# Key pages loaded whole over 128 partitions, and turned probabilities sorted by position on TensorE

## The reference

```python
def _sample_attention(l, q, k_new, v_new, qi, ki_new, wi, cache_k, cache_v, cache_kidx, page_table):
    ...
    scores = _index_scores(qi, wi, ki_all)
    qpos = past + jnp.arange(T)
    causal = jnp.arange(L)[None, :] <= qpos[:, None]
    scores = jnp.where(causal[None], scores, -jnp.inf)
    _, idx = lax.top_k(scores, topk)            # topk = 256 of 1028 positions
    ...
    k_sel = jnp.where(is_past, cache_k[l, phys_page, offset].astype(k_new.dtype), k_new[bidx, nidx])
    v_sel = jnp.where(is_past, cache_v[l, phys_page, offset].astype(v_new.dtype), v_new[bidx, nidx])
    return _sparse_attend(q, k_sel, v_sel, valid)

def _sparse_attend(q, k_sel, v_sel, valid):
    s = jnp.einsum('bthd,btkhd->bthk', q, k_sel) * (HEAD_DIM ** -0.5)
    s = jnp.where(valid[:, :, None, :], s, -jnp.inf)
    p = jax.nn.softmax(s, axis=-1)
    return jnp.einsum('bthk,btkhd->bthd', p, v_sel)
```

## Time and profile before

| | |
|---|---|
| median of three runs | 1252.48 us (1248.2 to 1258.6) |
| the profiled execution | 1256.65 us, span 1254.8 us |
| PE busy | 1146.8 us (91%) |
| DVE, ACT, POOL busy | 641.2, 318.7, 354.4 us |
| mean granted TensorE clock | 0.953 |
| moved by DMA | 171.53 MB, mean 137 GB/s |

### The profile page before, as it was taken

One profiled execution on the slowest core, in us unless ns is written; L12 is line 12 of the kernel. 1 busy time (PEld: TensorE's weight loads), 2 busy tenths in 40 slices (PEclk: granted clock), 3 DMA queues, 4 the chain that ended last, 5 costly groups with the idle time before them and its releaser, 6 DMA issues.

```text
span 1254.8 us, 29323 instructions
## 1 busy us (share of the span) xinstructions
PE 1146.8 (91%) x11340; PEld 1065.1 (85%) x11340; DVE 641.2 (51%) x1173; ACT 318.7 (25%) x593; POOL 354.4 (28%) x150
## 2 busy tenths in 40 slices
PE   6999999999999999999957878887887899999995
PEld 6988889999999999999947767777766789999992
DVE  3566658875475575624554434624622752232326
ACT  4333334223233322323211111111111242212110
POOL 2433323333343343334202131121220313333320
PEclk8999999999999999999988988888889899999996
DMA  7542142332332333354049997997999958222203
GB/s 242 137 106 77 48 121 69 93 85 77 86 106 81 86 91 96 89 139 119 24 113 253 255 211 191 242 225 196 239 210 224 244 169 261 83 84 80 70 0 143
DMA packets 201900, 171.53 MB, mean 137 GB/s; under 512 B 22034, under 2 KB 182730, under 8 KB 200562
## 3 DMA queue, kind: packets, MB, share of 16 engines
q1 hardware_dynamic: 188410, 161.41, 49.3%
q10 hardware_dynamic: 13376, 8.53, 2.3%
HBM read 159.57 MB, written 9.90 MB: 135 GB/s over the span
## 4 chain that ended last, share of the span: by engine, by line
PE 70%; SPq 11%; DMA 8%; DVE 6%; issue 5%; ACT 1%; DVEq 0%; ACTq 0%
PE acc L1132 58%; SPq L454 4%; DMA kPage<-in_cache_k 4%; SPq L502 3%; DMA hist<-in_state_pool 3%; PE bank L1190 2%; PE bank L1307 1%; DVE scoreP L1755 1%; PE bank L1326 1%; DVE top L1751 1%; PE acc L1459 1%; PE bank L1432 1%; PE acc L1545 1%; SPq L457 1%; DMA xnat<-in_x_prompt 1%
## 5 line engine op out<-in xcount | busy, mean ns | idle before, releaser
L659 POOL TENSOR_TENSOR wL<-rawW,wH 128x1024 fp32r<-128x1024 f32 (+1 forms) x146 | 354.2, 2428 | 853.3 <-ACT wH L681 853.3
L1132 PE MATMUL acc<-actH,wH 128*128 128x272 f32 (+1 forms) x2304 | 499.1, 298 | 19.7 <-ACT raw L1005 16.2
L1132 PE MATMUL acc<-actH,wL 128*128 128x272 f32 (+1 forms) x2304 | 481.8, 291 | 0.0
L1132 PE MATMUL acc<-actL,wH 128*128 128x272 f32 (+1 forms) x2304 | 481.2, 291 | 0.0
L1132 PEld LDWEIGHTS acc<-actH,wH 128*128 128x128 f32 (+1 forms) x2304 | 366.7, 191 | 50.7 <-issue 49.0
L1132 PEld LDWEIGHTS acc<-actL,wH 128*128 128x128 f32 (+1 forms) x2304 | 367.4, 191 | 0.0
L1132 PEld LDWEIGHTS acc<-actH,wL 128*128 128x128 f32 (+1 forms) x2304 | 364.8, 191 | 0.0
L681 ACT ACTIVATE wH<-rawW 128x1024 fp32r<-128x1024 f32 (+1 forms) x146 | 153.3, 1054 | 269.5 <-PE acc L1132 235.0
L1860 DVE STREAM_TRANSPOSE kPage<-kPage 128x1024 f32<-128x1024 f32 x30 | 37.4, 1246 | 135.4 <-DMA kPage<-in_cache_k 135.3
L2095 DVE SCALAR_TENSOR_TENSOR y<-y,bank 128x512 f32 (+1 forms) x16 | 11.0, 688 | 123.3 <-PE bank L1609 121.4
L1432 PE MATMUL bank<-kPage,qBlock 128*32 128x64 f32 x1920 | 38.7, 239 | 31.1 <-DVE kPage L1861 27.2
(11 more groups left out here) (210 smaller groups left out, 906.6 us busy)
## 6 DMA issues: line engine op xcount, KB each, us to landing
rawW<-in_w_in SPq DMA_DIRECT2D x112, 512.0 KB, 3.9
vPage<-in_cache_v SPq DMA_DIRECT2D x64, 512.0 KB, 9.3
kPage<-in_cache_k SPq DMA_DIRECT2D x112, 256.0 KB, 6.4
rawW<-in_w_out SPq DMA_DIRECT2D x32, 512.0 KB, 3.9
y<-in_x_prompt SPq DMA_DIRECT2D x4, 1024.0 KB, 8.6
out_y_prompt<-y SPq DMA_DIRECT2D x8, 512.0 KB, 2.8
xnat<-in_x_prompt SPq DMA_DIRECT2D x2, 1024.0 KB, 8.3
xnat<-in_x_prompt ACTq DMA_DIRECT2D x2, 1024.0 KB, 11.5
```

Source lines behind the costliest of these rows:

```text
L659: pool.tensor_tensor(wL[:, slot, :, 0:width], rawW[:, slot, :, 0:width], wH[:, slot, :, 0:width].bitcast(F32), ALU.subtract).then_inc(stag ...
L1132: last = pe.matmul(acc[t.slot][0:width, e, 0:HT], w[:, u.slot, k, 0:width], a[:, kk, e * HT:(e + 1) * HT], start=(half == 0 and k == 0 and ...
```

## The change

A key page is loaded whole, one DMA over all 128 partitions as a value page is, so a unit is two DMAs in place of four, and both page numbers are read before the wait for the buffer. Side s now holds positions 32 s to 32 s + 31 of each page. The scores of page p so stand in columns 32 p to 32 p + 31 of `probS`, with the sides on rows. `dropD` is written to match, in runs of 32 numbers rather than 128. The two transposes of the probabilities become 32 products: for page p and side s the stationary operand is the 32 columns of page p, the moving operand 32 columns of the identity that pick the rows of side s, and the result goes to partitions 32 s to 32 s + 31. `probST` is then position by page by row, and `value_page` reads its four columns from there.

Three things are moved. The first two units of "a" are taken in the order 1, 0, and DVE turns them earlier, between softmaxes of the last two heads. SP issues a half-tile of weights (`unit(4)`) ahead of the mask instead of behind it. SP issues `pool_loads(0)` right behind the first mask, ahead of the wait for `c_done` and of the first values and keys.

```diff
 BLOCK = QUARTERS * SIDES * STREAK
+FIRST = (1, 0, 2, 3)
 TRI = [0, 128, 384, 768, 1280]
...
             probSTn = sb("probSTn", [NS, P], F32, s)
-            probST = sb("probST", [P, 2, P], F32, s)
+            probST = sb("probST", [P, PAGES, NS], F32, s)
             pooledS = sb("pooledS", [P, 2, NS], F32, s)
...
             uN = hist[0:NS]
-            outS = probST[:]
+            outS = probST[:].rearrange("p a t -> p (a t)").rearrange("p (a d) -> p a d", a=HALF)
             qAll = mixed[:, KC - 2:KC, :].rearrange("p k t -> p (k t)")[:, 0:SIDES * H * NS].rearrange("p (j n) -> p j n", j=SIDES)
...
             def first_key_part(unit, e):
-
-                dst, at = first_keys(unit, e), STREAK * (2 * (unit % 2) + e)
-                for side in range(SIDES):
-                    page = page_number(ck, SIDES * (unit // 2) + side)
-                    sp.dma_start(dst[STREAK * side:STREAK * (side + 1), :],
-                                 ck[ds(page, 1), at:at + STREAK, :].rearrange("a p n -> p (a n)")).then_inc(first_k_in[unit], 16)
+                load_page(ck, first_keys(unit, e), page_number(ck, 2 * unit + e), first_k_in[unit])

...
                 i, at = (0, 0) if g is None else (g, g)
+                pages = [page_number(ck, (2 * at + x) * PAGES + (2 * n + e)) for e in range(2)]
                 sp.wait_ge(k_done, 2 * UNITS * i + done)
-                for side in range(SIDES):
-                    page = page_number(ck, (2 * at + x) * PAGES + (SIDES * (n // 2) + side))
-                    rows_of = ck[ds(page, 1), 2 * STREAK * (n % 2):2 * STREAK * (n % 2 + 1), :]
-                    sp.dma_start(kPage[STREAK * side:STREAK * (side + 1), 1 - n % 2, :, :, :].rearrange("p e h d -> p e (h d)"),
-                                 rows_of.rearrange("a (e p) n -> p (a e) n", e=2)).then_inc(k_in[n % 2], 16)
+                for e in range(2):
+                    load_page(ck, kPage[:, 1 - n % 2, e, :, :].rearrange("p h d -> p (h d)"), pages[e], k_in[n % 2])

...
                 for a in range(HALF):
-                    sp.dma_start(dropD[side, a, :, 0:HP].rearrange("r (h n) -> r h n", h=2),
-                                 scoreS[:, 0:PAST].rearrange("r (h s n) -> r h s n", h=2, s=SIDES)[:, :, side, :]
+                    sp.dma_start(dropD[side, a, :, 0:HP].rearrange("r (p n) -> r p n", p=PAGES),
+                                 scoreS[:, 0:PAST].rearrange("r (p s n) -> r p s n", p=PAGES, s=SIDES)[:, :, side, :]
                                  ).then_inc(drop_out, 16)
...
                          outside[0:NS, 0:NS].unsqueeze(1).to_broadcast([NS, (SIDES - 1) * HALF, NS])).then_inc(drop_out, 16)
-            mask(0, None)
             unit(4)
+            mask(0, None)
+            pool_loads(0)
             sp.wait_ge(c_done, 1)
...
             value_page(0, 0)
-            key_unit(1, 0, 1)
+            key_unit(1, 0, FIRST.index(0) + 1)
             value_page(0, 1)
             unit(5)
-            pool_loads(0)
             value_page(0, 2)
...
                     src = bank_wait(act, b)
-                    act.activation(probST[:].rearrange("p a r -> p (a r)"), src[:, 0:2 * P], ACT.Copy)
+                    act.activation(probST[:].rearrange("p a r -> p (a r)"), src[:, 0:PAGES * NS], ACT.Copy)
                     out_of(b, probSTn[:], src[0:NS, 2 * P:3 * P])
...
                 i, x, b = 0 if g is None else g, "abc".index(X), bb(f"S{X}", g)
-                pe.wait_ge(k_turned, 2 * UNITS * i + UNITS * x + n + 1)
-                if n == 0:
+                at = n if x else FIRST.index(n)
+                pe.wait_ge(k_turned, 2 * UNITS * i + UNITS * x + at + 1)
+                if at == 0:
                     pe.wait_ge(pad_ready, 2 * i + x + 1)
...
             copied(TILE_C + 31)
-            for n in range(UNITS):
+            for n in FIRST:
                 key_products("a", n)
...
                     stand_alone(pe)
-                    for n in range(2):
-                        pe.transpose(dst[:, n * P:(n + 1) * P], probS[:, n * P:(n + 1) * P], ident)
+                    for p in range(PAGES):
+                        for side in range(SIDES):
+                            pe.matmul(dst[STREAK * side:STREAK * (side + 1), p * NS:(p + 1) * NS], probS[:, p * STREAK:(p + 1) * STREAK],
+                                      ident.rearrange("p (j s r) -> p j s r", j=QUARTERS, s=SIDES)[:, :, side, :],
+                                      start=True, stop=True)
                     full(b, pe.transpose(dst[0:NS, 2 * P:3 * P], probS[:, HP:LP], ident))
...

-                    def column(h, side):
-                        at = h % QUARTERS * SPAN + (side * HALF + h // QUARTERS) * NT
+                    def column(h, step):
+                        at = h % QUARTERS * step + h // QUARTERS * NT
                         return slice(at, at + NT)
...
                     for h in range(H):
-                        end = products(h, probST[:, p // SIDES, column(h, p % SIDES)], vPage[:, v.slot, h, :], p == 0, False)
+                        end = products(h, probST[:, p, column(h, HALF * NT)], vPage[:, v.slot, h, :], p == 0, False)
                     end.then_inc(v_free[v.slot], 1)
...
                         for h in range(H):
-                            end = products(h, probSTn[:, column(h, 0)], vS[:, h, :], False, True)
+                            end = products(h, probSTn[:, column(h, SPAN)], vS[:, h, :], False, True)
                         full(o, end)
...
                 if X == "a":
-                    dve.wait_ge(first_k_in[n], 16 * 2 * SIDES)
+                    dve.wait_ge(first_k_in[n], 32)
                     parts = [first_keys(n, e) for e in range(2)]
                 else:
-                    dve.wait_ge(k_in[n % 2], 16 * SIDES * (4 * i + 2 * (x - 1) + n // 2 + 1))
+                    dve.wait_ge(k_in[n % 2], 32 * (4 * i + 2 * (x - 1) + n // 2 + 1))
                     parts = [kPage[:, 1 - n % 2, e, :, :].rearrange("p h d -> p (h d)") for e in range(2)]
...
                     rotated(1, qT, 0, i)
+                if late:
+                    keys_turned("a", FIRST[0])
                 softmax(0)
...
                     rotated(3, qT, 1, i)
+                    if late:
+                        keys_turned("a", FIRST[1])
                     gated(0, (2, 3))
...
                     own.wait()
-                    keys_turned("a", 0)
                     queries(0)
-                    keys_turned("a", 1)
-                    keys_turned("a", 2)
                 if i:
...
                         own.wait()
-            keys_turned("a", 3)
+            for n in FIRST[2:]:
+                keys_turned("a", n)
             dve.wait_ge(c_done, 1)
```

More of the change, by code:

```diff
@@ L581, in _ @@
                          outside[0:NS, 0:NS].unsqueeze(1).to_broadcast([NS, (SIDES - 1) * HALF, NS])).then_inc(drop_out, 16)
+            unit(4)
             mask(0, None)
-            unit(4)
+            pool_loads(0)
             sp.wait_ge(c_done, 1)
```

## The result

The changed kernel took **1175.45 us** (median of 4 runs, 1175.03 to 1180.29) against 1253.22 us (median of 4 runs, 1248.2 to 1258.6) of the kernel before: ratio 0.9403, 95% interval 0.9359 to 0.9448. The forecast was 1182. Its forecast was 1186.65. Ratios are of fast runs alone: in the experiments a few runs of the kernel before lie over 1.5% above its fastest and are left out of them.

The account below looks back on a forecast made before the run. It took the DMA engines as fullest, PE next. Waits and clock 58 plus start 17 minus sorting 5 gave 70 us off the profiled 1256.65, so 1186.65; the forecast median was 1182, range 1162 to 1220.

Parts of the forecast that it names:

- The cause: Sample stage: a key byte loaded over 32 partitions costs the DMA engines twice a value byte, 208 against 407 GB/s.
- The waits: PE's waits in the groups shrink: 23 us at key products, 10 at later groups' history, 15 at new accumulators.
- The slow clock: Six quarter tiles after waits, slow at a low granted clock: 10 us of 11.9 us regained.
- The start: Start of the sample stage: mask and history come sooner, PE begins the first group near 647, not 665.3: 17 us.
- Sorting: Turns of the probabilities on PE: 32 small products replace two transposes, eight times, costing 5 us; bounds 2 and 117.
- the rule on drains: Skill's rule that changing the tiling mode drains TensorE: two more drains a sorting turn would make 5 us about 7.
- Small pieces: Dropped scores, eight DMAs writing 128-byte instead of 512-byte pieces: cost 1 us, inside the start's 17; bounds 0 and 27.
- The key turns among the softmaxes: Two key turns on DVE, moved among the last heads' softmaxes, could delay PE's transposes up to 2.5 us; counted as nothing.
- Full DMA engines at 255 GB/s: Rival: DMA engines stay the bound in the groups, each gaining only 10 to 14 us; 1198 to 1210 us; chance 0.25.
- "Nothing": Rival: waits on keys only pass to another order, leaving part of the start, under 12 us; 1241 to 1252; chance 0.06.
- dear small pieces: Rival at the start: 128-byte writes of the dropped scores cost the whole 27 us; 1208 us; chance 0.05.
- sorting without overlap: Rival on PE: sorting products do not overlap, 15.3 us a turn over eight turns; about 1294 us; chance 0.04.

Follow-up runs that it names:

- the second set: Experiments on one chip with their own runs of the kernel before; the changed kernel, timed there again without edits, took 1176.34 us, ratio 0.9407.

## Why the prediction was right, point by point

*The cause.* That a key byte over 32 partitions costs twice was read from two narrow windows; the runs with narrow and wide loads show the width as the cause of the gain in the time. What they do not show is why the width counts. That SP's shorter units need no large term of their own is shown by the four wide DMAs: twice the issues and half the row are 5 to 6 us of the 76. The DMA need was put at 69 and 80 us a group, key bytes alone becoming cheaper; it is 66.5 and 65.3, and the weights' packets became cheaper too, 29.4 ns in place of 35.6 (735 to 895 us). So PE's need and that of the DMA engines do not lie level, as the prediction had it: PE's is 10 us larger.

*The waits* (23 + 10 + 15 = 48 us). Key turns gave 22.8 us (27.2 to 4.4), the history of the later groups 10.7 (13.5 to 2.8, which is another wait), new accumulators 16.2. New waits took 5.5 (output) and 2.5 (ACT) back; with small ones the idle time fell by 45.0. That the history would still wait behind values was wrong: it lands in time in every group.

*The slow clock* (10 us). This term was mis-sized. I had counted only the six slow quarter tiles right behind a wait. PE's busy time fell by 16.3 us although the sorting added 4.6, so the same other products took 20.9 us less, with the clock at 1.00 in place of 0.88 to 0.90. Key products ran slow before as well, 38.7 us for 1920 records; now:
```profile
L1427 PE MATMUL bank<-kPage,qBlock 128*32 128x64 f32 x1920 | 33.8, 222 | 7.8 <-DVE kPage L1859 4.4 <-issue 3.4
```
Value products went from 43.5 to 38.2 us. The place to read it was PE's 82 busy us a group at that clock, not six rows of the chain.

*The start* (17 us). This term was mis-sized the other way. The first group does begin 14.7 us earlier, at 650.6 and not near 647. But after the first group only 3.8 us are left of it against the kernel with wide keys alone (7.8 us with the profile of the second set), or 5 to 9 with the two turns sorted in that group. The times agree: that kernel is 4.7 us slower and has no 4.6 us of sorting to pay, so the rest of the change, start included, is worth some 9 us. The step that failed is "So it begins the first group near 647 in place of 665.3", taken as a gain in full: the first group, which needs the same bytes by its end, gave about half of the early start back.

*The sum* (70 us, measured 76 between the profiles). In the ledger the start counts with its full 14.7 us, and what it gives back stands among the first group's waits: the clock then makes 10.9 us more than its term, the waits 3.0 and the start 2.3 less. Counted by what the start is worth, about 9, waits and clock made 72 us (76.3 and the 4.6 of sorting, less 9) where they were put at 58. Either way errors of opposite sign stand in the sum, and that the time came out within 7 us of the forecast is in part luck.

*Sorting* (5 us): 4.6. (The 7 us by the rule on drains was not worked out rightly: two more at 0.22 us a turn would make 3.5 us over eight turns, 8.5 in all.) *Small pieces* (1 us): 0.35. *The key turns among the softmaxes* (nothing): nothing, and their gain at the gating (4.9 us before, 0.5 now) did not outlast the first group either.

*The rivals.* Full DMA engines at 255 GB/s: the groups moved 275 to 291 GB/s at a share of 0.82 to 0.88, so only the first group is near that case. "Nothing" fell with the result, dear small pieces and sorting without overlap each with the run above that undid them.

*What would show it.* Key windows near 400 (391 to 393), share under 0.9, two issues a unit, PE's waits on keys and history together 9.7 us, a turn of about 1 us: as said. The pitch was 80.1 and 79.6 for the second and third group, 84.5 for the first.

## What to carry to other kernels

When the DMA engines count as full, divide bytes by time in windows where one kind of load is alone: a load that gets half the rate of its neighbour at the same row size differs from it in its shape. Here the repair was to let each DMA span all 128 partitions, though the consumer must then sort: 4.6 us paid for some 66. Read what a low granted clock costs from PE's busy time over the whole stage. And before an earlier start is counted, ask which loads the stage behind it needs, and when they can land.

## What the runs showed of the hardware that was not expected

- Two neighbouring quarters of the partitions in one DMA are hardly better than one while keys are alone: 216 to 244 GB/s over 64 partitions, 194 to 240 over 32, 391 to 396 over 128, all with rows of 4 KB. With the other loads among them the stage moves 232 GB/s over 64 and 214 over 32.
- Beside loads over part of the partitions other loads are slower: the weights' packets of 512 bytes took 39.9 ns beside keys over 32 partitions, 35.0 over 64 and 29.4 over 128 (means of 735 to 895 us).
- At full width, packets of 2 KB took 94.9 ns where packets of 4 KB took 183.0.
- The eight writes of the dropped scores land in 3.0 us in place of 1.8; with long pieces at the changed kernel's place they took 3.0 us too: the size of the piece was not the cause.
- 32 products, each with its own stationary of 32 columns, cost 0.57 us more than the two transposes of 128 that they replace.
